# Decode attention in a one-core decoder step: pages of K turned in 32x32 blocks on VectorE, with block-diagonal queries and selection matmuls

## The reference, cut to what matters

```python
def fox_sample(q, k_new, v_new, log_f_new, cache_k, cache_v, cache_logf, page_table):
    past_k = cache_k[page_table].reshape(B, -1, H_FOX, HEAD_DIM)
    past_v = cache_v[page_table].reshape(B, -1, H_FOX, HEAD_DIM)
    ...
    past_suffix = jnp.flip(jnp.cumsum(jnp.flip(past_lf, axis=1), axis=1), axis=1) - past_lf
    bias_k = jnp.concatenate([past_suffix, -g_new], axis=1)
    ...
    s = jnp.einsum('bqhd,bshd->bhqs', q, k).astype(jnp.float32) * ATTN_SCALE
    s = s + bias_q + bias_k
    p = jax.nn.softmax(s, axis=-1)
    return jnp.einsum('bhqs,bshd->bqhd', p.astype(v.dtype), v)
```

## Time and profile before

| | us |
|---|---|
| median of 3 runs | 2432.29 (2429.2 to 2434.31) |
| the profiled execution, its own time | 2430.75 |
| its span, first to last instruction | 2429.1 |
| TensorE busy | 2333.9 (96%) |
| VectorE busy | 1062.8 (44%) |
| ScalarE busy | 811.0 (33%) |
| GpSimd busy | 464.2 (19%) |

### The profile page before, as it was taken

The page is one execution under the profiler, slowest core; times in us unless marked ns, Lnnn a source line. Parts: engine busy times, 40 slices in busy tenths (PEclk is TensorE's granted clock), DMA queues, the critical chain, the costliest instruction groups (busy, mean ns, idle before and its releaser), DMA issues.

```text
span 2429.1 us, 45416 instructions
## 1 busy us (share of the span) xinstructions
PE 2333.9 (96%) x18348; PEld 2132.6 (88%) x18348; DVE 1062.8 (44%) x1446; ACT 811.0 (33%) x986; POOL 464.2 (19%) x876
## 2 busy tenths in 40 slices
PE   6999999999899999999989998999999999999998
PEld 6999999998766677666669997999999999999998
DVE  6443434433333333333326436554444444444444
ACT  3223232333433344334412334233332232323334
POOL 2120000002233333333311230211111111111110
PEclk8999999999999999999999999999999999999999
DMA  8474435536999999999876643877776766688894
GB/s 252 150 215 156 143 120 163 164 101 214 287 366 363 341 342 351 366 332 349 323 268 192 203 153 127 275 236 242 240 233 229 253 223 232 223 285 269 289 307 131
DMA packets 337905, 589.57 MB, mean 243 GB/s; under 512 B 17503, under 2 KB 279971, under 8 KB 334079
## 3 DMA queue, kind: packets, MB, share of 16 engines
q0 software_dynamic: 68112, 312.68, 36.5%
q1 hardware_dynamic: 269648, 274.86, 35.6%
HBM read 564.06 MB, written 113.06 MB: 279 GB/s over the span
## 4 chain that ended last, share of the span: by engine, by line
PE 83%; DMA 9%; issue 3%; DVE 3%; ACT 2%; POOL 1%; SPq 0%; POOLq 0%; DVEq 0%; ACTq 0%
PE ps L838 15%; PE ps L840 15%; PE ps L839 15%; PE ps L876 6%; PE ps L878 6%; PE ps L877 6%; DMA kraw<-in_cache_win_k 4%; PE ps L1066 3%; DMA kraw<-in_cache_fox_k 3%; PE ps L1071 2%; PE ps L1091 2%; PE ps L1055 2%; PE ps L1151 2%; PE ps L1057 2%; PE ps L1056 2%
## 5 line engine op out<-in xcount | busy, mean ns | idle before, releaser
L1692 DVE TENSOR_TENSOR w_lo<-raw,w_hi 128x2048 fp32r<-128x2048 f32 (+2 forms) x248 | 526.5, 2123 | 767.4 <-ACT w_hi L1359 767.4
L1359 ACT ACTIVATE w_hi<-raw 128x2048 fp32r<-128x2048 f32 (+2 forms) x248 | 435.6, 1756 | 1036.9 <-PE ps L840 735.6
L838 PE MATMUL ps<-act_hi,w_hi 128*128 128x320 f32 x1616 | 499.6, 309 | 2.0 <-DVE w_lo L1692 2.0
L840 PE MATMUL ps<-act_hi,w_lo 128*128 128x320 f32 x1616 | 499.3, 309 | 0.0
L839 PE MATMUL ps<-act_lo,w_hi 128*128 128x320 f32 x1616 | 499.3, 309 | 0.0
L876 PE MATMUL ps<-act_hi,w_hi 128*128 128x320 f32 x1008 | 317.5, 315 | 0.0
L878 PE MATMUL ps<-act_hi,w_lo 128*128 128x320 f32 x1008 | 311.5, 309 | 0.0
L877 PE MATMUL ps<-act_lo,w_hi 128*128 128x320 f32 x1008 | 311.4, 309 | 0.0
L838 PEld LDWEIGHTS ps<-act_hi,w_hi 128*128 128x128 f32 x1616 | 303.3, 188 | 2.5 <-DVE w_lo L1692 2.5
L839 PEld LDWEIGHTS ps<-act_lo,w_hi 128*128 128x128 f32 x1616 | 303.3, 188 | 0.0
L840 PEld LDWEIGHTS ps<-act_hi,w_lo 128*128 128x128 f32 x1616 | 303.3, 188 | 0.0
(11 more groups left out here) (381 smaller groups left out, 3760.1 us busy)
## 6 DMA issues: line engine op xcount, KB each, us to landing
raw<-in_w_gate_up SPq DMA_DIRECT2D x88, 1024.0 KB, 7.5
kraw<-in_cache_fox_k POOLq DMA_DIRECT2D x128, 512.0 KB, 6.5
vraw<-in_cache_fox_v POOLq DMA_DIRECT2D x128, 512.0 KB, 6.8
raw<-in_w_in SPq DMA_DIRECT2D x60, 1024.0 KB, 7.9
raw<-in_w_down SPq DMA_DIRECT2D x32, 1024.0 KB, 5.6
out_win_k_sample<-in_cache_win_k POOLq DMA_DIRECT2D x64, 510.0 KB, 5.9
out_win_v_sample<-in_cache_win_v POOLq DMA_DIRECT2D x64, 510.0 KB, 3.9
raw<-in_w_gate SPq DMA_DIRECT2D x52, 512.0 KB, 11.1
```

Source lines behind the costliest of these rows:

```text
L838: pe.matmul(ps[:, bk_, 0:T], w_hi[:, slot, k, :], xh[:, x_k, :], start=(k == k0), stop=False)
L840: mm = pe.matmul(ps[:, bk_, 0:T], w_lo[:, slot, k, :], xh[:, x_k, :], start=False, stop=(k == k1 - 1))
L1359: act.activation(w_hi[:, slot, 0:kt, :], raw[:, pslot, 0:kt, P * slot:P * slot + P], ACT.Copy).then_inc(hi_done, 1)
L1692: dve.tensor_tensor(w_lo[:, slot, 0:kt, :], raw[:, pslot, 0:kt, P * half:P * half + P], w_hi[:, slot, 0:kt, :].bitcast(F32), ALU.subtract) ...
```

## The change

The K pages of the paged cache are no longer turned by TensorE. VectorE turns each 128x1024 page by one instruction in 32x32 blocks straight from `kraw` to the new tile `kS` (`keys_f`). After it partition 32*t + d of a block holds value d of tokens 32*t to 32*t+31, so the queries stand in a block-diagonal tile `qb` (four quarters of the tokens by 8 queries are 32 columns), copied by `fox_queries` from `qs`. Scores need 32 matmuls of 64 columns with 32 stationary columns for two pages, in place of 8 of 256 with 16. They fill all 128 rows: a row is head, quarter and query. Bias and scores have 512 columns for each half of the heads, and the bias of a batch is one DMA of 128 rows x 1024. Maximum and sum have to be joined over four rows each, which takes two small turns by TensorE and a few small VectorE instructions for each (`turn_top`, `spread_top`, `turn_sum`, `spread_sum`). `turn_fox` puts the probabilities back by 32 matmuls against a selection matrix `selx` where there were 4 transposes, one step later. The window blocks are handled as before.

```diff
+    c[np.arange(P), C_SELX + 32 * part + 8 * head + query] = 1
...
-        fb = sb("fb", [P, PAST], F32, X0 + 16384)
-        fs = sb("fs", [P, PAST + DT], F32, X0 + 24576)
-        qf = sb("qf", [P, HF, 2 * DT], F32, Y0 + 5984)
+        kS = sb("kS", [P, 2, 2, 1024], F32, X0)
+        fb = sb("fb", [P, 2, 512], F32, X0 + 16384)
+        fs = sb("fs", [P, 2, 512 + DT], F32, X0 + 20480)
+        qs = sb("qs", [P, 4, HF, NS], F32, X0 + 24640)
...
+        qb = sb("qb", [P, HF, 4, 32], F32, Y0 + 2784)
...
-            for q in range(DT):
-                pool.dma_start(fbd[:, q].rearrange("h b (g t) -> (b g) h t", t=P), fbx[:]).then_inc(fb_st, 16)
+            pool.dma_start(fbn.rearrange("b g h t -> (b g) (h t)"), fbx[:].rearrange("p h t -> p (h t)")).then_inc(fb_st, 16)
+            pool.wait_ge(acc_free, U_FQ + HF + 2)
+            pool.dma_start(qsc, sT[:, 0:HF, :].rearrange("p h n -> p (h n)")).then_inc(fb_st, 16)
...
+                    if old_s < NPG:
+                        pool.wait_ge(kf_ok, old_b * NPG + old_s + 1)
...
+            for b in range(DB):
+                for e in range(2):
+                    pool.dma_start(fb1[b].rearrange("j q e g t -> e (j q) g t")[e],
+                                   fbn[b, :, 4 * e:4 * e + 4].rearrange("g j (q t) -> (j q) g t", q=4)).then_inc(fb_st, 16)
...
+            pool.dma_start(fbd.rearrange("b r i n -> (b r) i n"),
+                           fb1.rearrange("b j q e g t -> (b j q) (e g t)").unsqueeze(1).broadcast_to([DB * 16, DT, 1024])).then_inc(fb_st, 16)
...
+            for part in range(4):
+                pool.dma_start(qs[32 * part:32 * part + 32].rearrange("p q h n -> p q (h n)"),
+                               qsc.rearrange("(q p) n -> p q n", p=32)).then_inc(pd_c, 16)
+            pool.dma_start(selx[:], consts[:, C_SELX:C_SELX + P]).then_inc(pd_c, 16)
...
-                for j in range(4):
-                    rows = fbd[2 * j:2 * j + 2, :, b, :].rearrange("h q n -> (h q) n")
-                    pool.dma_start(fb[32 * j:32 * j + 2 * DT, :], rows).then_inc(fb_ld, 16)
+                pool.dma_start(fb[:].rearrange("p e n -> p (e n)"), fbd[b].rearrange("r i n -> (r i) n")).then_inc(fb_ld, 16)
...
-                pe.wait_ge(qf_ok, b + 1)
                 wait_pos(pe, pf_ev, 4 * b)
-                for h in range(HF):
-                    j = 32 * (h // 2)
-                    mm = pe.matmul(ps[j:j + 2 * DT, 4, 0:DT], qf[:, h, :], sT[:, NQ + h, DT * b:DT * b + DT],
-                                   start=(h % 2 == 0), stop=(h % 2 == 1), **mmx)
-                mm.then_inc(fnew_sc, 1)
-
-            def fox_scores(b, g):
-
-                pe.wait_ge(ke_a, b * KPG + 2 * g + 2)
-                pe.wait_ge(ke_b, narrow(b, 2 * g + 1) + 1)
-                pe.wait_ge(f_ev, 9 * b + 1 + g)
+                wait_pos(pe, red_ok, 5 * b)
                 for e in range(2):
                     for j in range(4):
-                        mm = pe.matmul(ps[32 * j:32 * j + 2 * DT, 4, 0:256], qf[:, 2 * j + e, :], kT[:, g % 2, 2 * j + e, :],
-                                       start=(e == 0), stop=(e == 1), **mmx)
+                        h = 4 * e + j
+                        mm = pe.matmul(ps[32 * j:32 * j + DT, 4, DT * e:DT * e + DT], sT[:, h, DT * b:DT * b + DT],
+                                       sT[:, NQ + h, DT * b:DT * b + DT], start=(e == 0), stop=(e == 1), **mmx)
+                mm.then_inc(fnew_sc, 1)
+
+            def fox_scores(b, g):
+
+                if g == 0:
+                    pe.wait_ge(qf_ok, b + 1)
+                pe.wait_ge(kf_ok, b * NPG + 2 * g + 2)
+                pe.wait_ge(f_ev, 9 * b + 1 + g)
+                for q in range(4):
+                    for e in range(2):
+                        for j in range(4):
+                            c = 32 * (4 * (4 * e + j) + q)
+                            mm = pe.matmul(ps[32 * j:32 * j + 32, 4, 64 * e:64 * e + 64], qb[:, 4 * e + j, q, :],
+                                           kS[:, g % 2, :, c:c + 32], start=(q == 0 and e == 0), stop=(q == 3 and e == 1), **mmx)
                 mm.then_inc(sc_done, 1)
 
+            def turn_top(b):
+
+                pe.wait_ge(red_ok, 5 * b + 1)
+                pe.transpose(ps[0:2, 4, 0:P], fm[:, b % 2, 18:20], ident[:]).then_inc(red_tr, 1)
+
+            def spread_top(b):
+
+                pe.wait_ge(red_ok, 5 * b + 2)
+                pe.transpose(ps[:, 4, P:P + 2], top2[:], ident[0:2, 0:2]).then_inc(red_tr, 1)
+
+            def turn_sum(b):
+
+                pe.wait_ge(pf_ev, 4 * b + 4)
+                pe.wait_ge(f_exp, 2 * b + 2)
+                pe.transpose(ps[0:2, 4, 0:P], fm[:, b % 2, 22:24], ident[:]).then_inc(red_tr, 1)
+
+            def spread_sum(b):
+
+                pe.wait_ge(red_ok, 5 * b + 4)
+                for j in range(4):
+                    mm = pe.matmul(ps[32 * j:32 * j + 2 * DT, 4, P:P + 1], sum2[:, 16 * j:16 * j + 16], ones[0:2, 0:1],
...
-                pe.wait_ge(f_exp, 2 * b + 1 + r // 2)
-                wait_pos(pe, f_ev, 9 * b + 9) if r == 0 else pe.wait_ge(pf_ev, 4 * b + r)
+                if r == 0:
+                    pe.wait_ge(pd_c, 96)
+                    pe.wait_ge(f_exp, 2 * b + 2)
+                else:
+                    pe.wait_ge(pf_ev, 4 * b + r)
                 for k in range(4):
                     s = 4 * r + k
-                    mm = pe.transpose(ps[:, 4, P * k:P * k + P], fs[:, P * s:P * s + P], ident[:])
+                    for e in range(2):
+                        c = 64 * k + 32 * e
+                        for q in range(4):
+                            mm = pe.matmul(ps[32 * q:32 * q + 32, 4, c:c + 32], fs[:, e, 32 * s:32 * s + 32], selx[:, 32 * q:32 * q + 32],
+                                           start=(k == 0 and e == 0), stop=(k == 3 and e == 1), **mmx)
...
-                    if kb is not None and n < KPG:
+                    if kb is not None and NPG <= n < KPG:
                         transposes(kb, n)
+                    if kb is not None and n == 18:
+                        spread_top(kb)
                     gate_part(q, n)
+                    if vb is not None and n == 0:
+                        turn_sum(vb)
+                    if vb is not None and n == 1:
+                        spread_sum(vb)
...
-                        if 19 <= n < 23:
-                            turn_fox(kb, n - 19)
+                        if n == 17:
+                            turn_top(kb)
+                        if 20 <= n < 24:
+                            turn_fox(kb, n - 20)
...
+                for part in range(4):
+                    rows = slice(32 * part, 32 * part + 32)
+                    ins = dve.tensor_copy(qb[rows, :, :, DT * part:DT * part + DT], qs[rows, :, :, DT * b:DT * b + DT].rearrange("p q h n -> p h q n"))
                 ins.then_inc(qf_ok, 1)
+
+            def keys_f(b, s):
+
+                n = b * KPG + s
+                dve.wait_ge(k_ld[n % KRING], loads_before(b, s, KRING))
+                if s % 2 == 0 and b * 12 + s // 2 >= 2:
+                    dve.wait_ge(sc_done, scored_before(b, s // 2))
+                dve.transpose(kS[:, s // 2 % 2, s % 2, :], kraw[:, n % KRING, :]).then_inc(kf_ok, 1)
...
-                biased(fs[:, 256 * g:256 * g + 256], ps[:, 4, 0:256], fb[:, 256 * g:256 * g + 256], fm[:, b % 2, g:g + 1]).then_inc(f_ev, 1)
+                now = slice(64 * g, 64 * g + 64)
+                for e in range(2):
+                    ins = biased(fs[:, e, now], ps[:, 4, 64 * e:64 * e + 64], fb[:, e, now], fm[:, b % 2, 9 * e + g:9 * e + g + 1])
+                ins.then_inc(f_ev, 1)
...
+                dve.wait_ge(red_tr, 4 * b + 1)
+                top = row2[:, 0, :].rearrange("r (j i) -> r j i", j=4)
+                link(dve.tensor_reduce(top, by_part(ps[0:2, 4, 0:P]), AX, ALU.max, negate=True))
+                dve.tensor_copy(by_part(top2[:]), top.unsqueeze(3).broadcast_to([2, 4, DT, 4])).then_inc(red_ok, 1)
...
-                        if n < KPG and n != NPG:
+                        if n < NPG:
+                            keys_f(kb, n)
+                        elif NPG < n < KPG:
...
+                        if n == 17:
+                            fox_top(kb)
+                        if n == 18:
+                            fox_top_rows(kb)
...
+                            fox_sum(vb)
+                        if n == 1:
+                            fox_sum_rows(vb)
```

166 lines of the change are left out of this document (98 added, 68 removed).

## The result

| | before | after |
|---|---|---|
| median of the runs | 2433.93 us (7 runs, 2429.2 to 2435.28) | 2443.59 us (7 runs, 2438.23 to 2446.92) |
| profiled execution, its span | 2430.75 us, 2429.1 us | 2446.75 us, 2445.2 us |
| ratio | | 1.0042, 95% interval 1.0028 to 1.0056 |

The changed kernel is slower by 0.4%, some 10 us. The profiled execution of after is at the upper end of its runs, so the two traces are 16 us apart; a stretch of the traces tells where time lies, the ratio how much it is.

The account below looks back on a forecast made before the run. TensorE (76.8 us) and DMA (73.2 us) demands, close together, were taken to bound each 80.6 us decode batch; -36 (seven batches) - 5 (first batch) + 3 (start) = -38 us gave 2394 us, range 2355 to 2438 us.

Parts of the forecast that it names:

- the sum for a batch: Decode batch: TensorE 76.8 - 13.6 (page turns removed) + 3 + 5 = 71.2 us, DMA 70.7; period 75.5 us, -5.1 us.
- The DMA demand, 73.2 us: Decode batch before the change: 28.1 MB at 400 GB/s take 70.2 us, plus some 3 us for the bias dip.
- Scores, +0: Score matmuls on TensorE: a group of 64 instructions takes 0.88 us again, as the old 16 did.
- Putting back, +1.0 us: Turns of the probabilities on TensorE: 64 instructions at 13 ns, 0.84 us against 0.59, +1.0 us for four.
- VectorE's queue, +5 us of waits for TensorE: A batch's end: page turns and copies in VectorE's in-order queue make TensorE wait, +5 us for a batch.
- Bias, -2.5 us: Bias load of each batch: one DMA of 128 rows removes the 3 us dip, 0.5 us kept as unsure.
- Start, +3 us: Start of the first batch: late `qs` load, and bias behind a K load that waits for the first turn, +3 us.
- First batch, -5 us: First batch: 8 page pairs could save 12 us, but K waits and gate weights stay, so about half, -5 us.
- Stationary loads bind: Rival, 64-instruction groups: loading 32 stationary columns costs 28 ns, batch 83 to 84 us, 2456 us; chance 0.14.
- The batch's end takes back what is won: Rival, batch's end: TensorE waits 10 us and more behind VectorE's next pages; at 14 us, about 2440 us; chance 0.12.
- DMA alone bounds: Rival, whole batch: TensorE's slack lets the rings run at full rate, 70.7 + 1.5 us a batch, 2368 us; chance 0.2.
- periods above 80 us: Sign of a wrong forecast: first scores of successive batches over 80 us apart, where 75.5 us was expected.

Follow-up runs that it names:

- light_before: The kernel before, with the second half of each K and V page's row not loaded once the rings are filled: 2405.7 us, ratio 0.9884.
- dead_turns: The changed kernel with 8 dead full-width turns of the identity per page put back on TensorE: 2453.53 us, ratio 1.0086.
- half_turn: The changed kernel with half of the selection matmuls that put the probabilities back left out (heads 4 to 7): 2418.47 us, ratio 0.9923.
- keys_early: The changed kernel with VectorE's queue reordered: next batch's pages turned earlier round a batch's end, query copies moved to step 18: 2433.52 us, ratio 0.9989.
- bias_16rows: The changed kernel with each batch's bias loaded by eight DMAs of 16 rows instead of one of 128: 2456.61 us, ratio 1.0085.
- bias_first: The changed kernel with the first batch's bias loaded ahead of the fourth page of K instead of behind it: 2437.81 us, ratio 1.0007.
- turn_spread: The changed kernel with each turn's 32 selection matmuls in groups of four between gate matmuls instead of one burst: 2485.18 us, ratio 1.0201.
- early_late: The changed kernel with next pages first in VectorE's queue, first bias load earlier, three of four probability turns moved into the next batch's pages: 2421.34 us, ratio 0.9935.

## Why the forecast was wrong, point by point

**The failed step** is the sum for a batch: "As now, the batch takes some 3.8 us more than the larger" of the two whole-batch demands, 71.2 and 70.7 us. A batch isn't one pool of work. Its pages are bound by transfers, its windows and end by TensorE (the windows with transfers close behind), and seven blocks of ring (3.7 MB, 9 us at 400 GB/s) carry little from one to the other. The 13.6 us were taken from the pages. Of the 43.9 us there TensorE alone needs 41.0 (light_before), and the transfers need about the 44 us that the changed kernel takes with TensorE idle for a fifth of them. With the second floor where it is, lowering the first brings nothing. dead_turns measured the worth of the 13.6 us as 1.3 us for each batch. The window stretch and the end, where the kernel's time is TensorE's, got more to do.

**The DMA demand, 73.2 us, was mis-sized** too. It took the rate of the fullest 6 us, 400 GB/s, for all 28.1 MB. Over six whole batches the share was 0.99 at 350 GB/s; by the fullest share, 1.04, the demand was 80.6 x 0.99 / 1.04 = 76.7 us.

**Scores, +0:** right, 0.89 us a group. **Putting back, +1.0 us:** the work was no more than before (0.58 to 0.75 us a turn against 0.59), but 2.1 us of gaps in short instructions stood in no term. Half of the bursts cost 3.6 us for each batch (half_turn).

**VectorE's queue, +5 us of waits for TensorE:** the place was right, and so was the price of the block transpose (1.24 us, booked at 1.2). The wait of TensorE was smaller, about 1.8 us for each batch (the last two rows of its waits above, with 1.3 us in front of `L1114`, are 12.5 us in 7 batches); the price was paid in transfers: K and V loads that went 4 us later, 1.6 us for each batch (keys_early). The forecast had named "K's ring is now freed by VectorE" and booked nothing for it.

**Bias, -2.5 us:** right in kind; 1.3 us the other way round (bias_16rows). **Start, +3 us:** right in kind, 7.1 us in size; 4.9 us of it was the order of the bias behind the fourth K load (bias_first), the rest no run explains. **First batch, -5 us:** 72.1 to 71.5 us, -0.6: its K and weight loads kept it. **Elsewhere, 0:** from the eighth batch's first scores to the output projection the traces lose another 1.7 us, which no run explains.

**The rivals.** "Stationary loads bind" fell: 64 instructions in 0.89 us are 14 ns each. The Trainium skill, "TensorE: Matmul & The Clock Gate", section "Wait — 56ns, not 53.3ns?", has starts never closer than about 25 ns; this case's trace doesn't agree where four strips work side by side, and the measurement decides. "The batch's end takes back what is won" gave 2440 us and comes nearest in number, and its place is half of the truth. "DMA alone bounds" was true of the pages, with a demand too small by some 4 us. The last sentence of the forecast, that it would be wrong with "periods above 80 us" or a falling clock, came true in both; but of the two the period is what counts: with the clock brought back (dead_turns) the loss stayed. Above 80 us was a weak sign, though: the kernel before had 80.6.

**The sum of what was measured**, for each batch against the kernel before: +1.3 (ratio: 10 us in 8). The gaps are +2.1, the loads held back +1.6, the bias -1.3, and the freed turns at most -1.3; with the start's 7 us in 8, +0.9, this makes +2.0. Each of these is good to some 0.6 us, so the difference is within what these runs can tell. What the clock costs at the end is not separated from the first two.

## What to carry to other kernels

Cut the period where the bound changes hands, and read busy time and DMA share of each piece before a saving is booked: work taken off an engine counts only in the pieces which that engine bounds, and only down to the other's floor there. A rate that holds for 6 us isn't the rate of a batch. When an engine becomes the one that frees a ring, its queue belongs to the transfers' path: look at what stands in it ahead of the freeing instruction, and put that instruction first. Here the three moves (pages first, bias first, turns where TensorE waits) took the change from 1.0042 to 0.9935. And count instructions as well as their work: many short ones can stall an engine that is nowhere short of data.

## What the runs showed of the hardware

- Short matmuls outrun what feeds TensorE. Bursts of 64 instructions in 0.6 us were broken by gaps of 0.3 to 3.8 us with nothing to wait for, 21 us in all in the changed kernel, 14 us in the kernel before once it had such bursts, 4 us when long matmuls stood between them. TensorE's instructions come in packets of 16 KB, 256 at a time, 103 packets in the kernel before and 134 in the changed one (8,164 matmuls and weight loads and 31 packets more), and every one of these gaps ends 1.2 to 1.6 us after such a packet has landed.
- 64 matmul instructions with 32 stationary columns, on four strips, start within 0.57 us when 32 columns stream (9 ns each) and 0.88 us when 64 do (14 ns each).
- A change from full-width matmuls to a strip group and back costs 0.32 us (turn_spread).
- While transfers into 16 rows are under way the DMA engines are as busy and move 258 GB/s (bias_16rows) or 201 GB/s (before), where page loads reach 404.
- TensorE's granted clock was 0.94 over six batches of the changed kernel, with TensorE idle for 84 of 492 us, against 0.99 with 30 of 484 us before. Within one page stretch it was as low as 0.86 (in early_late, TensorE busy for 36.95 of 46.40 us), a part of it at the lower of its two levels, 1.2 GHz. At that level a group of scores takes 1.62 us instead of 0.88, as 8 of the changed kernel's 64 groups do, in pages where TensorE has time to spare. dead_turns raised the mean over the run from 0.974 to 0.987, and the time did not fall.
